# Twelve residual updates: the weight split's last nine GpSimd slabs on VectorE, the affine step on ScalarE, and fillers between the transposes

## What is computed

```python
# first block, per layer l
h = modulate(rmsnorm(x, norm_mix[l]), sh_m, sc_m)       # h * (1 + scale) + shift
x = x + g_m[:, None, :] * mix
h = modulate(rmsnorm(x, norm_ffn[l]), sh_f, sc_f)
x = x + g_f[:, None, :] * swiglu(h, ffn_w_gate[l], ffn_w_up[l], ffn_w_down[l])
# second block, per layer i
f = swiglu_2(rmsnorm_2(h, g[0]), ffn_gate[i, 0], ffn_up[i, 0], ffn_down[i, 0])
h = h + MACARON * rmsnorm_2(f, g[1])
mix = hybrid_mixer(rmsnorm_2(h, g[2]), ...)
h = h + rmsnorm_2(mix, g[3])
f = swiglu_2(rmsnorm_2(h, g[4]), ffn_gate[i, 1], ffn_up[i, 1], ffn_down[i, 1])
h = h + MACARON * rmsnorm_2(f, g[5])
gate = jax.nn.sigmoid(rmsnorm_2(h, g[6]) @ w_ple_gate[i])
h = h + rmsnorm_2((p[i] @ w_ple[i]) * gate, g[7])
```

## Time and profile before

| | |
|---|---|
| median of 3 runs | 1861.29 us (1858.51 to 1867.29) |
| the profiled execution | 1860.23 us, span 1858.6 us |
| TensorE busy (matmul) | 1742.7 us, 94% |
| VectorE busy | 1231.0 us, 66% |
| ScalarE busy | 893.7 us, 48% |
| GpSimd busy | 163.8 us, 9% |
| mean granted TensorE clock | 0.97 |
| weight subtractions on GpSimd | 12, 54.8 us |
| transposes of x (line 593) | 176 |

### The profile page before, as it was taken

How to read it: one execution, slowest core, us unless ns; L and a number is a source line. 1 busy time by engine, 2 the same in 40 slices (tenths; PEclk the granted TensorE clock), 3 DMA queues, 4 the chain that set the end, 5 groups by cost and what they waited for, 6 DMA issues and landing times.

```text
span 1858.6 us, 30112 instructions
## 1 busy us (share of the span) xinstructions
PE 1742.7 (94%) x11898; PEld 1605.8 (86%) x11898; DVE 1231.0 (66%) x1622; ACT 893.7 (48%) x1211; POOL 163.8 (9%) x172
## 2 busy tenths in 40 slices
PE   7987899989899998999998999988999999899997
PEld 4975799979799998999896899978999897799986
DVE  7889887767865546555576665556555567765555
ACT  4572543345544335334476543345434467643445
POOL 2023211121110001000111100001000103100000
PEclk9998999999999999999999999998999999999998
DMA  9775598858345453555340454543555531355451
GB/s 378 291 276 204 207 357 309 312 197 304 145 170 203 181 182 125 203 191 191 131 178 1 170 204 181 181 147 138 192 183 183 188 137 69 125 181 181 181 199 39
DMA packets 61926, 353.82 MB, mean 190 GB/s; under 512 B 6522, under 2 KB 9738, under 8 KB 27792
## 3 DMA queue, kind: packets, MB, share of 16 engines
q1 hardware_dynamic: 40064, 281.24, 41.7%
q0 software_dynamic: 18384, 66.66, 10.0%
q10 hardware_dynamic: 3392, 4.72, 0.7%
HBM read 349.45 MB, written 3.15 MB: 190 GB/s over the span
## 4 chain that ended last, share of the span: by engine, by line
PE 80%; DVE 10%; ACT 4%; issue 3%; DMA 2%; DVEq 0%; POOL 0%; SPq 0%; ACTq 0%; POOLq 0%
PE bank L535 23%; PE bank L536 23%; PE bank L537 23%; PE bank L569 1%; PE bank L568 1%; PE bank L567 1%; ACT w_hi L1034 1%; PE bank L593 1%; PE bank L707 1%; DVE x L1638 1%; DMA raw<-in_stream 1%; PE bank L728 1%; DVE w_lo L1507 1%; DVE shared L2057 1%; DVE shared L1528 1%
## 5 line engine op out<-in xcount | busy, mean ns | idle before, releaser
L535 PE MATMUL bank<-a_hi,w_hi 128*128 128x256 f32 x2648 | 755.3, 285 | 7.1 <-DVE a_lo L1679 3.7
L536 PE MATMUL bank<-a_lo,w_hi 128*128 128x256 f32 x2648 | 751.2, 284 | 0.0
L537 PE MATMUL bank<-a_hi,w_lo 128*128 128x256 f32 x2648 | 751.1, 284 | 0.0
L535 PEld LDWEIGHTS bank<-a_hi,w_hi 128*128 128x128 f32 x2648 | 510.5, 193 | 11.1 <-issue 7.9
L536 PEld LDWEIGHTS bank<-a_lo,w_hi 128*128 128x128 f32 x2648 | 510.4, 193 | 2.9 <-issue 0.7
L537 PEld LDWEIGHTS bank<-a_hi,w_lo 128*128 128x128 f32 x2648 | 509.9, 193 | 0.0
L1778 DVE TENSOR_TENSOR w_lo<-raw,w_hi 128x2048 fp32r<-128x2048 f32 x144 | 330.0, 2292 | 258.5 <-ACT w_hi L1160 258.5
L1160 ACT CAST w_hi<-raw 128x2048 fp32r<-128x2048 f32 x144 | 273.9, 1903 | 269.7 <-PE bank L537 269.7
L1507 DVE TENSOR_TENSOR w_lo<-raw,w_hi 128x2048 fp32r<-128x2048 f32 x110 | 251.7, 2294 | 130.8 <-ACT w_hi L1034 130.6
L1034 ACT CAST w_hi<-raw 128x2048 fp32r<-128x2048 f32 x122 | 231.1, 1906 | 92.3 <-PE bank L537 85.2
L535 PE MATMUL bank<-w_hi,hid_hi 128*128 128x512 f32 x548 | 215.9, 394 | 5.9 <-DVE hid_lo L2203 3.1
(11 more groups left out here) (241 smaller groups left out, 2010.2 us busy)
## 6 DMA issues: line engine op xcount, KB each, us to landing
raw<-in_stream SPq DMA_DIRECT2D x266, 1024.0 KB, 4.8
shared<-in_mods POOLq DMA_DIRECT2D x102, 512.0 KB, 6.6
grow<-in_rows POOLq DMA_DIRECT2D x12, 512.0 KB, 3.9
work<-in_mods POOLq DMA_DIRECT2D x8, 512.0 KB, 9.2
bias_rows<-work ACTq DMA_DIRECT2D x1, 2048.0 KB, 21.2
x<-in_x_t SPq DMA_DIRECT2D x1, 1024.0 KB, 5.8
x<-in_x_d ACTq DMA_DIRECT2D x1, 1024.0 KB, 4.9
work<-bias_rows ACTq DMA_DIRECT2D x1, 1024.0 KB, 16.7
```

Of the source, the lines that this page charges most:

```text
L535: pe.matmul(out, w_h, v_h, start=start, stop=False, skip_group_check=True)
L536: pe.matmul(out, w_h, v_l, start=False, stop=False, skip_group_check=True)
L537: return pe.matmul(out, w_l, v_h, start=False, stop=stop, skip_group_check=True)
```

## The change

- `POOL_LOW` keeps only the three slabs of the recurrence's output product. The nine others go to VectorE's `split_to`, where they stand just ahead of the update (for u2(0, 3) just behind it), and the waits and subtractions leave GpSimd's list.
- `turn_x` puts 3, 6 and 3 fillers between the four pieces; the four fillers behind the last piece are gone. The fillers ahead of the first piece stay.
- In the affine step ScalarE makes `affine` in pairs of chunks straight from the banks and then casts `a_hi` from it; VectorE only subtracts. For A_KV it also copies the banks to `sq` afterwards, for A_MIX1.
- At U_FFN0, VectorE's columns and scale for A_KV stand behind the update instead of ahead of it, and TensorE's reduction for A_MIX1 stands behind the slab pair instead of ahead of it. At U_LRU the second slab of the pair is subtracted ahead of the update.
- The wait of TensorE for `xc_ready` ahead of the second gate row is gone, and the other count on it is 4 instead of 8.

```diff
--- before.py
+++ after.py
@@ -475,7 +475,6 @@
             mod_load(*range(42, 48))
-            low(B_FFN0 + 1)
             row_load(U_FFN0)
...
@@ -595,10 +588,12 @@
                     if t == 1 and c % 2:
                         mm.then_inc(turned, 1)
 
-            def turn_x(u, src, ready):
+            def turn_x(u, src, ready, b=1):
 
                 for p in range(4):
                     turn_piece(src, ready, p, (f_ready, 4 * u + 4) if p == 1 else None)
+                    if p < 3:
+                        keep_warm(6 if p == 1 else 3, b)
 
             def residual(u):
                 return lambda p: (x_ready, x_at(u, p))
@@ -806,27 +801,25 @@
             def turn_normed(u, warm=6, b=1):
 
                 keep_warm(warm, b)
-                turn_x(u, f_one, normed_x(u))
-                keep_warm(4, b)
+                turn_x(u, f_one, normed_x(u), b)
 
             pe.wait_ge(grow_ready, 2)
             mod_reduce(G_B0, 3, range(8))
             turn_normed(U_LRU)
 
-            def second_row(g, u):
+            def second_row(g):
                 def emit():
-                    pe.wait_ge(xc_ready, 4 * (u + 1))
                     gate_row(g, 1, 4)
                 return emit
 
-            ffn(0, B_FFN0, A_FFN0, second_row(G_B0, U_LRU))
+            ffn(0, B_FFN0, A_FFN0, second_row(G_B0))
 
 
             mod_reduce(G_KV, 1)
             turn_normed(U_FFN0, b=2)
-            mod_reduce(G_MIX1, 3)
             need_slab(B_KV + 1)
             slab_pair((B_KV, B_KV + 1), (bank[0], bank[1]), before(APPLY_CHUNKS, A_KV))
+            mod_reduce(G_MIX1, 3)
             for i in range(2, 4):
                 need_slab(B_KV + i)
                 if i == 3:
@@ -1116,19 +1105,34 @@
                         token_rsqrt(u, p // 2, ss(p), (ss_ready, ss_at(u) + p + 1))
                 if ap is None:
                     return
+                act.wait_ge(scale_ready, ap + 1)
                 for b4 in range(4):
                     act.wait_ge(turned, 4 * u + b4 + 1)
-                    act.copy(sq[:, 2 * b4:2 * b4 + 2, :].rearrange("p c s -> p (c s)"), bank[4 + b4][:, :]).then_inc(xc_ready, 1)
-                affine_hi(ap, scale, shift)
-
-            def affine_hi(ap, scale, shift, free=None):
-
-                for c in range(CH):
+                    affine_pair(ap, b4, lambda m: bank[4 + b4][:, m * S:(m + 1) * S], scale, shift)
+                if ap == A_KV:
+                    for b4 in range(4):
+                        act.copy(sq[:, 2 * b4:2 * b4 + 2, :].rearrange("p c s -> p (c s)"), bank[4 + b4][:, :]).then_inc(xc_ready, 1)
+
+            def affine_pair(ap, b4, src, scale, shift, free=None):
+
+                for m in range(2):
+                    c = 2 * b4 + m
+                    act.activation(affine[:, c, :], src(m), ACT.Identity, scale=scale(c), bias=shift(c)).then_inc(tmp_ready, 1)
+                for m in range(2):
+                    c = 2 * b4 + m
                     if free is not None:
 
                         act.wait_ge(*free(c))
                     act.wait_ge(tmp_ready, affine_at(ap) + c + 1)
-                    act.activation(a_hi[:, c, :], sq[:, c, :], ACT.Identity, scale=scale(c), bias=shift(c)).then_inc(nh_ready, 1)
+                    act.copy(a_hi[:, c, :], affine[:, c, :]).then_inc(nh_ready, 1)
+
+            def affine_hi(ap, scale, shift, free):
+
+                act.wait_ge(scale_ready, ap + 1)
+                for b4 in range(4):
+                    act.wait_ge(xc_ready, b4 + 1)
+                    act.wait_ge(*free(2 * b4 + 1))
+                    affine_pair(ap, b4, lambda m: sq[:, 2 * b4 + m, :], scale, shift, free)
 
             def a_out(c):
                 return a_hi[:, c, :]
@@ -1651,21 +1655,12 @@
                         else:
                             dve.tensor_scalar(half(f_one, t, h), half(x, t, h), r_tok(t), None, ALU.mult).then_inc(xn_ready, 1)
 
-            def affine_low(ap, scale, shift, ahead=1):
+            def affine_low(ap):
 
                 at = before(APPLY_CHUNKS, ap)
-
-                def low(c):
+                for c in range(CH):
                     dve.wait_ge(nh_ready, at + c + 1)
                     dve.tensor_tensor(a_lo[:, c, :], affine[:, c, :], a_hi[:, c, :].bitcast(F32), ALU.subtract).then_inc(nl_ready, 1)
-
-                for c in range(CH):
-                    dve.wait_ge(xc_ready, XC_AT[ap] + c // 2 + 1)
-                    dve.tensor_scalar(affine[:, c, :], sq[:, c, :], scale(c), shift(c), ALU.mult, ALU.add).then_inc(tmp_ready, 1)
-                    if c >= ahead:
-                        low(c - ahead)
-                for c in range(max(CH - ahead, 0), CH):
-                    low(c)
 
             def normed(ap, n, src, gain, hi, lo, shift=None, at=0, ahead=1):
 
@@ -1952,22 +1947,20 @@
             split_to(B_FFN0 + 1)
             mod(G_B0, 6)
             mod(G_B0, 7)
+            split_to(B_FFN0 + 2)
             add_gated(U_LRU, B_LOUT + 4)
-            split_to(B_FFN0 + 2)
             mod_columns(G_B0, 3, 0, 8)
             scale_of(1, G_B0, 0, COL_AT["norm_ffn"])
-            dve.wait_ge(scale_ready, 2)
-            affine_low(A_FFN0, lambda c: scale1[:, CH + c:CH + c + 1], lambda c: modcol(G_A0, CH + c))
+            affine_low(A_FFN0)
             split_to(B_FFN0 + 3)
             ffn(0, B_FFN0)
 
 
             split_to(B_KV + 2)
+            add_gated(U_FFN0, B_FFN0 + 3 * FJ - 1)
             mod_columns(G_KV, 1)
             scale_of(2, G_KV, CH, COL_AT["kv_norm"])
-            dve.wait_ge(scale_ready, 3)
-            add_gated(U_FFN0, B_FFN0 + 3 * FJ - 1)
-            affine_low(A_KV, lambda c: scale1[:, 2 * CH + c:2 * CH + c + 1], lambda c: modcol(G_KV, c))
+            affine_low(A_KV)
             split_to(B_KV + 3)
             mod_columns(G_MIX1, 3)
             scale_of(3, G_MIX1, CH, COL_AT["norm_mix"] + CH)
@@ -2256,9 +2244,7 @@
 
 SUMS_BEFORE = {G_B0: (0, 1), G_KV: (1, 1), G_MIX1: (1, 2), G_B1: (0, 5)}
 MOD_AHEAD = [34, 35]
-POOL_LOW = [B_LOUT + i for i in range(1, 4)] + [B_FFN0 + 1, B_KV + 1, B_FFN1 + 1]
-for _l in range(LAYERS2):
-    POOL_LOW += [base2(_l) + 1, base2(_l, M_MIX) + 1, base2(_l, M_FFN) + 1]
+POOL_LOW = [B_LOUT + i for i in range(1, 4)]
 GATE_ENDS = (1, 3, 4)
 ATANH_LAST = 17
 LAM_STEPS = 5 + (ATANH_LAST - 3) // 2 + 4
```

More of the change, by code:

```diff
@@ L841, in queries @@
                 feature_slab(B_Q + i, bank[i], before(APPLY_CHUNKS, A_MIX1) if i == 0 else None).then_inc(slab_done, 1)
-            pe.wait_ge(xc_ready, 8)
+            pe.wait_ge(xc_ready, 4)
             mod_reduce(G_A1, 4, range(8, 16))
@@ L1977, in _ @@
             mod(G_B1, 1)
-            dve.wait_ge(scale_ready, 4)
-            affine_low(A_MIX1, lambda c: scale1[:, 3 * CH + c:3 * CH + c + 1], lambda c: modcol(G_MIX1, c), ahead=CH)
+            affine_low(A_MIX1)
             split_to(B_KV + 6)
```

16 lines of the change are left out of this document (2 added, 14 removed).

## The result

The changed kernel takes 1844.86 us (median of 7 runs, 1840.32 to 1846.26) against 1858.51 for the kernel before on the same chip (7 runs, 1852.99 to 1867.29): a ratio of 0.9918, 95% interval 0.9894 to 0.9942. It is faster by 0.6 to 1.1%, where I had forecast 1842 us and 1834 to 1855. The profiled execution took 1844.51 us, with a span of 1842.9 against 1858.6 before: 15.7 us less, where the sum of the prediction had 19.7.

The account below looks back on a forecast made before the run. TensorE's products bound the kernel (busy 94% of the span), leaving its waits at landings, the residual updates between product phases. Savings of 5.3 + 13.2 + 1.2 = 19.7 us from 1860.23 gave 1840.5, stated as 1842 us, range 1834 to 1855.

Parts of the forecast that it names:

- rival A: Fillers are only delay: four second-block landings give -0.5 to +0.5 us each, not 10.2 in sum; 1852 us, chance 0.19.
- (5): Landings idle before the first transpose: MOBA +0.6, FFN1 +0.4, LRU +0.2 us, row starting half clock, ending full; sum 1.2.
- rival C: Half clock through transposes, fillers and into products at every landing: 23 us slower, 1884; 4.7 per landing against forecast; chance 0.06.
- Part 1, the stalls: GpSimd's landing subtractions to VectorE: updates sooner by 1.5 us (MOBA, FFN1), 0.8 to 0.9 (four second-block), 3.74 near 1280.
- part 4: Second-block landings, fillers between transposes keeping the clock: 2.2, 1.9 plus 0.8, 3.1, 2.85, 2.3 us; sum 13.2.
- Part 2, the affine step: ScalarE reads banks itself: first a_hi after some 1.3 us, against copies of 2.05; only latency to the first chunk counts.
- Part 3, FFN0: New order at FFN0: products start 9.0 us sooner, the exposed reduction costs 3.65; net 5.3 us.
- the sign that I had named for being wrong: Landings with fillers take over 6 us from first transpose to first product, with the clock there at 0.5.
- the other signs: VectorE stalls gone; FFN0's x near 390, slab products 9 us sooner; clock 1.00 near 400 and at two landings like 1041.
- B (1835): Rival: at the landings, stalls count in full and the clock holds; 26 us sooner, 1835 us, chance 0.10.
- D (no effect): Rival: no effect, if x is not the release at landings and something unseen comes last; chance 0.03.
- The rule weighed: Near 909.5: part-filled stretches, gaps not over 1.4 us, cost the clock and filling keeps it; the skill blames idle gaps.

Follow-up runs that it names:

- e1: Kernel before with only the nine weight-slab subtractions moved from GpSimd to VectorE; 1842.0 us, ratio 0.9905.
- e11: e5 with VectorE's two weight subtractions moved ahead of its wait for the bias transfer; 1842.61 us, ratio 0.9896.
- e12: Control: e3 with VectorE's two weight subtractions moved ahead of its wait for the bias transfer; 1836.68 us, ratio 0.986.
- e5: e3 with the order at FFN0 put back: columns and scale ahead of the update, reduction ahead of the slab pair; 1847.91 us, ratio 0.992.
- e3: Changed kernel with four fillers behind the last piece, as before the change, and none between the pieces; 1837.92 us, ratio 0.9871.
- e4: Kernel before with only the fillers changed: 3, 6 and 3 between the pieces, the four behind the last gone; 1866.44 us, ratio 1.0029.
- e10: e9 with VectorE's two weight subtractions moved ahead of its wait for the bias transfer; 1826.26 us, ratio 0.98.
- e7: e3 with more fillers ahead of the first piece: LRU 18, MOBA 28, FFN1 40, near 1286 38; 1837.09 us, ratio 0.9884.
- e8: e6 and e7 together, plus 5 and 3 fillers behind pieces 0 and 1 at four second-block landings; 1836.02 us, ratio 0.985.
- e9: e8 with fewer fillers ahead of the transposes: 16, 16, 25 and 27; 1830.28 us, ratio 0.9824.
- e6: e3 with FFN0's exposed modulation reduction replacing ten fillers: 9 columns ahead of the transposes, 7 behind; 1839.24 us, ratio 0.9877.

## Why the prediction was right, and where it was wrong

**The total** (1844.86 against 1842, direction and range right) comes from parts that were not all right. Against the sum of 19.7 the spans differ by 15.7; the run took 1842.9 of span instead of the 1838.9 that this sum gives. The median of before was 1858.51 in the comparison, not 1861.29, so the gain by the medians, 13.7 us, is 5.7 short of the 19.3 forecast: the total looks nearer than the parts were. The measured terms, each the difference of the gaps of before and after in the table: FFN0 9.0 less the reduction, LRU -0.9, MOBA +0.2, FFN1 -0.5, the five of the second block 0.9, 1.9, 1.4, 1.9 and 1.7. Half clock behind the gaps, which the change ended, adds to the last five; counted from the landing's last product to the last of the phase behind it, they give 1.4, 2.7, 1.8, 2.7 and 2.15, in sum 10.8 where I had 2.2, 2.7, 3.1, 2.85 and 2.3, in sum 13.2. Counted in the same way MOBA gives 0.8 (I had 0.6), FFN1 -0.5 (0.4) and LRU -0.3 (0.2). Three sums in the text on record are slightly off and change no forecast: rival A's 10.2 is 10.05, the lower bounds of (5) and of 1286 together move the sum by -10.5 and not -9, and six landings at rival C's price end 0.48% slower, not over 0.5.

**Part 1, the stalls: right, and larger than I made it within the sum.** VectorE's two groups never exceed 0.694 and 0.159 us. First transposes come 1.6 us sooner at MOBA and FFN1 (I said 1.5), 3.7 sooner near 1286 (3.7) and 0.5 to 1.0 sooner at the other four (0.8 to 0.9). But e1 shows what I did not work out: this part alone brings 17 to 19 us. Nearly all that part 4 claims for the fillers near 1041 and 1615 (gaps of 9.7 to 7.3 and 9.4 to 7.3 us) comes with it, with the fillers where they were, since the clock does not fall there once the first transpose comes 1.0 us sooner. It also shows that GpSimd's subtraction was what stalled VectorE: in e1 the data and the work stay the same, only the engine that does it changes, and the operations of 5.09, 2.48 and 3.89 us are back at 0.69 and 0.16 at most.

**Part 2, the affine step:** my "nothing" beyond the first chunk is not contradicted. e11 differs from e1 in it, in the place of one subtraction at LRU, in the wait that is gone and in the edit at the bias wait, and takes 1842.6 against 1842.0 us. No run has this part alone. Its gap at MOBA is 1.1 us shorter (10.2 against 11.4), which the medians do not resolve.

**Part 3, FFN0: right.** Products came 9.0 us sooner by the gaps and the clock is 1.00 there. The reduction was exposed: from the first product to the last one at MOBA it is 90.56 us after and 87.01 before, 3.55 more, against its 3.65. Net 5.4 against my 5.3; e11 and e12 say 5.9 by the medians and 6.6 by the stretch. What I had not seen is the bias transfer: in e5, e3 with the old order, another 6 us are lost to it.

**Part 4, the fillers between pieces: the step that failed.** It is mis-sized by 2.4 us in the sum, and what it gained it owes mostly to part 1. I had reasoned that the clock, kept full by them, pays for them. The clock was kept at all four landings of the kind at 1041, where e3 keeps it at two; I had asked for two. But the price was left on the path: "products at 1045.8" assumed 3.6 us behind the second piece, and the profile has that (1036.69 to 1040.41, 3.7), and with it the gap of 7.75 us that I had forecast. Yet the same landing with the fillers behind takes 7.33 us against 7.75 if the clock holds, and 8.4 to 8.8 if it does not. Over the four, after has 31.5 us of gap and e3 31.8: break-even, not a gain. Near 1286 I took 3.1 "for the clock is back before the row of transposes ends". It is, but only just: half clock covers 6.0 us of it, to 1279.0, and the row ends at 1280.5. Measured are 1.8 by the lead, and e3's gap is 2.3 us shorter.

**Part 5:** "the row starts half and ends full" came true at FFN1 and was again priced too well (-0.5 for +0.4): half clock covers 703.6 to 709.0 of a row that ends at 710.8. At LRU (-0.9 in the gap for +0.2) and MOBA (+0.2 for +0.6) the clock falls 0.8 us behind the start of the first transpose, for 3.4 us. At LRU, MOBA, FFN1 and near 1286 it takes 7.0, 7.0, 7.5 and 7.7 us from the first transpose to the first product, partly at half clock: the sign that I had named for being wrong, at four of nine landings, while the other signs all came out right.

**The rivals.** A (fillers only delay) is closer than my forecast in what the fillers are worth: e3 and e4 show it from both sides. It was wrong on the total (1852) because the clock did not fall near 1041 and its like, as it had claimed. C, the slower end, is what happened at FFN1 in small. B (1835) and D (no effect) lie outside the measured interval.

**The rule weighed.** In e3 at the landing near 1481 the clock falls at 1463.8 although TensorE had been busy for 1.76 of the 3.40 us before, with no idle time over 1.35 us; the same landing in e10, with 5 and 3 fillers in the idle times, keeps it. A row of TensorE's timeline and the windows of e3, then the window of e10:

```profile
1463.17 0.63 PE L586 MATMUL bank<-ident,x 128*128 128x128 f32 x4 [1.35 <-DVE shared L2047]
```
```profile
1460.40:1463.80 3.40, 1.76 (x13) 1.13 (x11) 3.29 (x10) 0.30 (x1) 0.37 (x1) 1.00 0.63 263
1463.80:1467.20 3.40, 2.70 (x14) 2.70 (x14) 2.41 (x5) 1.97 (x6) 0.16 (x1) 0.50 0.48 154
```
```profile
1449.00:1457.00 8.00, 6.78 (x51) 5.71 (x50) 7.05 (x20) 3.58 (x12) 0.53 (x1) 1.00 0.53 196
```

So short idle times in series can cost the clock here, but they do not always: e12 has the same waits between its pieces at this landing as e3 (0.28, 1.35 and 0.70 us) and keeps it. Over the four landings near 905, 1041, 1481 and 1615, the eight kernels with no filler between the pieces and no stall (e1 to e3, e5 to e7, e11, e12) have a fall at 16 of 32, inside the gap or right behind it, among them all eight near 905 and none near 1041; the four kernels with fillers between them (after, e8 to e10) have none at 16. The Trainium skill's page "TensorE: Matmul & The Clock Gate", Part 1, names a long idle gap as the cause, and for one other kernel frequent short idle times between groups of matmuls; these rows agree with the second.

**What stays open.** Falls that no landing explains (near 975 and 1000 us after the change, near 1526 and 1550 in e10), 3.4 us each, I have not traced. The one near 975 stands at the same place in eleven of the fourteen profiles and is absent in e4, e9 and e10. Whether such falls differ between runs of one kernel no second profile shows, but the mean clock goes with the time: the runs of e8 have 0.986 at 1826.40 us and 0.981 at 1839.15. Why the bias transfer takes 8 to 24 us I know only by when: it goes with the order at FFN0, modulation and weight loads run beside it, and none was taken away.

## What to carry to other kernels

Put work that only keeps TensorE's clock where TensorE waits anyway, and count it: as many fillers as the wait holds ahead of the first of a row of dependent transposes, and between them no more than the waits there hold (here 5 and 3), since each one beyond that delays all that follows. Before crediting a bundle of edits, run each alone: here moving nine subtractions off GpSimd gave most of the gain, the order at FFN0 some 5 to 7 us, and the fillers between the transposes, as they were set, were a loss. And where a local gain does not arrive, look for the next wait on the same engine, up to 50 us on: a transfer with other work queued behind its wait was cured by turning the two round.

## What the hardware showed that I had not expected

GpSimd's memory sets, which only write, lie beside a VectorE subtraction and leave it at its length (the timeline of the changed kernel), while GpSimd's subtraction, which reads (4.49 us from 1279.55 in the kernel before), held an operation of 0.15 us for 3.89 us.

```profile
227.21 2.28 DVE L1511 TENSOR_TENSOR w_lo<-raw,w_hi 128x2048 fp32r<-128x2048 f32 x1
...
227.50 3.58 POOL L483 MEMSET shared<- 128x2048 f32 x2
```

And one 1 MB transfer took 8.4 us in e3, issued at 431.83 us, and 22.5 us in e6, issued at 431.70.
